# Attention slots of a two-block transformer kernel: outputs read one slot earlier, output units in halves

## What is computed

```python
def even_mixer(...):                       # layer 0; h_lat and h_ctx are 256 rows each
    qa, ka, va, qb, kb, vb = heads(h_lat)  # projections, RMS norms; the same for h_ctx
    qa = rope_2d(qa, row, col)
    ka = rope_2d(ka, row, col)
    o_a = window_attention(qa, ka, va, ka_c, va_c, a_sink)
    o_b = neighbourhood_attention(qb, kb, vb, kb_c, vb_c, b_rpb, rows_n)
    y_lat = jnp.concatenate([o_a, o_b], axis=-1) @ w_out
    ...                                    # y_ctx: the same weights over the context's attention
def odd_mixer(...):                        # layer 1, the latent mixer, no y_ctx
    ...
    y_lat = blockwise_dense_attention(q, k, v, kc, vc, scale) @ w_out
x = x + g1 * y_lat
```

## Time and profile before

| | us |
|---|---|
| runs before: lowest, median, highest of 3 | 2153.28, 2156.61, 2159.62 |
| the profiled execution's own time | 2161.3 |
| its span | 2159.5 |
| TensorE busy | 2067.6 |
| VectorE busy | 1548.4 |
| ScalarE busy | 929.7 |

### The profile page before, as it was taken

One profiled execution on the slowest core, in us unless ns is written; L12 is line 12 of the kernel. 1 busy time (PEld: TensorE's weight loads), 2 busy tenths in 40 slices (PEclk: granted clock), 3 DMA queues, 4 the chain that ended last, 5 costly groups with the idle time before them and its releaser, 6 DMA issues.

```text
span 2159.5 us, 37888 instructions
## 1 busy us (share of the span) xinstructions
PE 2067.6 (96%) x14296; PEld 1767.8 (82%) x14296; DVE 1548.4 (72%) x2708; ACT 929.7 (43%) x1553; POOL 30.0 (1%) x60
## 2 busy tenths in 40 slices
PE   7999999999999999899998889999999999899998
PEld 6889978889889998789975667788887875579987
DVE  7776768776887767888756566767787565767854
ACT  5554645554565544465524444321111234454332
POOL 0000000000000000000000000000000000000000
PEclk9999999999999999999999999999999999999999
DMA  7665525665554642355521111224545522003453
GB/s 277 252 223 186 190 77 196 253 248 167 201 182 167 218 149 98 137 194 180 196 100 59 40 40 62 101 97 156 194 158 210 197 78 81 18 35 124 183 182 139
DMA packets 50513, 326.48 MB, mean 151 GB/s; under 512 B 5360, under 2 KB 8688, under 8 KB 17264
## 3 DMA queue, kind: packets, MB, share of 16 engines
q1 hardware_dynamic: 42480, 266.62, 34.7%
q0 software_dynamic: 7936, 58.53, 7.5%
HBM read 324.07 MB, written 1.05 MB: 151 GB/s over the span
## 4 chain that ended last, share of the span: by engine, by line
PE 82%; DVE 12%; issue 3%; ACT 3%; DVEq 0%; DMA 0%; ACTq 0%; SPq 0%
PE psum L2221 14%; PE psum L2166 9%; PE psum L2167 8%; PE psum L2168 8%; PE psum L2222 7%; PE psum L2278 4%; PE psum L2279 4%; PE psum L2280 4%; PE psum L2774 3%; DVE w_lo L1219 2%; PE psum L2635 1%; PE psum L2775 1%; PE psum L2158 1%; PE psum L2299 1%; ACT w_hi L712 1%
## 5 line engine op out<-in xcount | busy, mean ns | idle before, releaser
L712 ACT ACTIVATE w_hi<-raw 128x1024 fp32r<-128x1024 f32 (+1 forms) x542 | 515.1, 991 | 605.6 <-PE psum L2168 366.3
L1219 DVE TENSOR_TENSOR w_lo<-raw,w_hi 128x1024 fp32r<-128x1024 f32 (+1 forms) x534 | 589.7, 1145 | 158.9 <-ACT w_hi L712 144.8
L2221 PE MATMUL psum<-h_both,w_hi 128*128 128x512 f32 x1344 | 476.5, 399 | 4.8 <-DVE rope_tmp L1269 3.6
L2222 PE MATMUL psum<-h_both,w_lo 128*128 128x256 f32 x1344 | 376.1, 280 | 0.0
L2221 PEld LDWEIGHTS psum<-h_both,w_hi 128*128 128x128 f32 x1344 | 252.3, 188 | 69.1 <-DVE rope_tmp L1269 3.7
L2166 PE MATMUL psum<-h_both,w_hi 128*128 128x256 f32 (+1 forms) x792 | 255.3, 322 | 7.6 <-DVE x_res L1433 2.0
L2222 PEld LDWEIGHTS psum<-h_both,w_lo 128*128 128x128 f32 x1344 | 253.5, 189 | 0.0
L2167 PE MATMUL psum<-h_both,w_hi 128*128 128x256 f32 (+1 forms) x792 | 251.8, 318 | 0.0
L2168 PE MATMUL psum<-h_both,w_lo 128*128 128x256 f32 (+1 forms) x792 | 251.6, 318 | 0.0
L2278 PE MATMUL psum<-g_both,w_hi 128*128 128x256 f32 x704 | 201.8, 287 | 1.2 <-DVE w_lo L1219 1.2
L2279 PE MATMUL psum<-g_both,w_hi 128*128 128x256 f32 x704 | 199.1, 283 | 0.0
(11 more groups left out here) (405 smaller groups left out, 3565.5 us busy)
## 6 DMA issues: line engine op xcount, KB each, us to landing
raw<-in_weights SPq DMA_DIRECT2D x207, 1024.0 KB, 4.8
raw_ada<-in_ada POOLq DMA_DIRECT2D x48, 1024.0 KB, 5.1
raw<-in_weights SPq DMA_DIRECT2D x64, 704.0 KB, 4.1
arena<-in_rpb POOLq DMA_DIRECT2D x1, 2048.0 KB, 12.3
arena<-in_fox_c POOLq DMA_DIRECT2D x1, 1696.0 KB, 9.5
const_region<-in_latent_c POOLq DMA_DIRECT2D x1, 1335.0 KB, 6.1
const_region<-in_even_c POOLq DMA_DIRECT2D x1, 1191.0 KB, 8.4
x_res<-in_x_lat SPq DMA_DIRECT2D x4, 256.0 KB, 7.2
```

Of the source, the lines that this page charges most:

```text
L712: nc.scalar.activation(wh[s][:, a], raw[s][:, a], ACT.Copy).then_inc(hi_ready, 1)
L1219: V.tensor_tensor(wl[s][:, a], raw[s][:, a], wh[s][:, a].bitcast(F32), ALU.subtract).then_inc(lo_ready, 1)
L2221: mm(psum[:, o, :], w_hi, h_both[:, :, k, 0:T], start=k == 0, stop=False)
L2222: ins = mm(psum[:, o, 0:T], w_lo, hh[:, k, 0:T], start=False, stop=k == DC - 1)
```

## The change

Two parts. In the even mixer VectorE's slot k reads the output of step k-2, not k-3; its place between shift and weighing stays. In the latent mixer an output unit is now two entries of the order, `out` with the first 12 matmuls and `done` with the other 12 and the semaphore. Units 0 to 3 stand in halves behind latent slots 11 to 18 (slots 35 to 42). VectorE makes the next panel's low half at `out` and updates the residual at `done`, both now after the weighing of their slot.

```diff
-                      9: (("spread", ("k", 6)),), 11: (("spread", ("k", 7)), ("out", 0)), 13: (("out", 1),),
-                      15: (("out", 2),), 16: (("out", 3),)}
+                      9: (("spread", ("k", 6)),), 11: (("spread", ("k", 7)),)}
             for k in range(19):
                 yield "slot", N_EVEN_STEPS + k
                 yield from behind.get(k, ())
+                if k > 10:
+                    yield ("out", "done")[(k - 11) % 2], (k - 11) // 2
             for q in range(4, 8):
                 yield "out", q
+                yield "done", q
...
                 for what, key in between:
-                    lat_unit(what, key)
+                    if what not in ("out", "done"):
+                        lat_unit(what, key)
                 if k < N_LAT:
                     step_weigh(k)
+                for what, key in between:
+                    if what in ("out", "done"):
+                        lat_unit(what, key)
...
-                if k >= 3:
-                    step_read(k - 3)
+                if 2 <= k < N_EVEN_STEPS + 2:
+                    step_read(k - 2)
...
+            def lat_out(out, s, k, m):
+
+                for kk in range(4):
...
+                    mm(o, w_hi, hh[:, y, 0:T], start=kk == 0, stop=False)
+                    mm(o, w_hi, hl[:, y, 0:T], start=False, stop=False)
+                    ins = mm(o, w_lo, hh[:, y, 0:T], start=False, stop=kk == 3)
+                return ins
...
-                        out = unit()
-                        for m in range(2):
...
-                        ins.then_inc(gemm_done, 1)
+                        out_half = unit()
+                        lat_out(out_half, s, k, 0)
+                    elif what == "done":
+                        lat_out(out_half, s, k, 1).then_inc(gemm_done, 1)
```

More of the change, by code:

```diff
@@ L2100, in lat_unit @@
                     dve.wait_ge(e_roped, 5 + pos.n("l_ropes", 1))
-                elif what == "out":
+                elif what == "done":
                     if k > 5:
@@ L2777, in mlp_latent @@
                 stage(4, 4, 1, 2, out_of)
+            def lat_out(out, s, k, m):
+                for kk in range(4):
+                    if k == 4 and m == 0:
+                        pe.wait_ge(st_y, 16 + 4 + kk + 1)
+                    w_hi, w_lo = wtile(s, kk, 2 * (k % 2) + m, TJ)
+                    y = 4 * (k // 4) + kk
+                    o = out[:, m * T:(m + 1) * T]
+                    mm(o, w_hi, hh[:, y, 0:T], start=kk == 0, stop=False)
+                    mm(o, w_hi, hl[:, y, 0:T], start=False, stop=False)
+                    ins = mm(o, w_lo, hh[:, y, 0:T], start=False, stop=kk == 3)
+                return ins
             def latent():
```

## The result

| | before | after |
|---|---|---|
| runs: lowest, median, highest of 4 | 2153.28, 2158.11, 2162.62 | 2135.60, 2137.98, 2141.38 |
| profiled execution, its span | 2161.3, 2159.5 | 2135.6, 2133.8 |
| ratio to the kernel before, 95% interval | | 0.9904 [0.9878, 0.9929] |

A forecast was written before the change was run, and what follows sets the result against it. TensorE's idle and low-clock stretches were taken as the bound. Even mixer -10.8, latent -3.4 and clock -4.2 gave -18.4 us: 2161.3 to 2142.9, less 4.7 for the slow profiled run, 2138; range 2132 to 2146.

The forecast's parts named there:

- What bounds the kernel: Whole kernel: TensorE, busy 96% of the span; only ending its idle or low-clock stretches saves time.
- Eight waits, -12.3: Even mixer, slots 4 to 14: value products' eight waits for the read of an output go, -12.3 us.
- Cover of 2.2 us: Even slots 4 and 18: weighing still ends 2.2 us or more before the transposes, despite the earlier read.
- New wait of +0.9 in slot 15: Even mixer: transposes in slot 15 newly wait about 0.9 us, shown in the profile after; bounds 0 and 1.1.
- Slot 6, +0.6: Even mixer: the earlier sum of squares in slot 6 meets ScalarE's square, +0.6 us; bounds 0 and 0.6.
- Latent, -3.8 and +0.4: Latent mixer: the 3.40 us wait and a third wait go, -3.8; breaks in four output units cost +0.4.
- Clock, -4.2: Half-clock stretches at 1235.6 and 1918.3, directly behind stalls that go, counted as won: 1.7 and 2.5 us.
- the first and third stretch: Half-clock stretches at 1235.6 (1.7 us) and 1918.3 (2.5 us), both expected to return to full clock.
- The second, counted as kept: Half-clock stretch at 1276.6, expected to stay because the spreads' waits ahead of it stay; 3.1 us more if it went.
- the clock that doesn't come back (2142): Rival, chance 0.15: waits go but low-clock stretches fall elsewhere; -14.2 us, so 2142.
- The displaced wait (2151): Rival, chance 0.06: even mixer's earlier reads make transposes late, eating its 10.8 us; -5.9 remains, so 2151.
- the closed loop (2165): Rival, chance 0.03: in VectorE's order each of 16 even-mixer reads holds the transposes 1.7 us; about +9, so 2165.

The follow-up runs named there:

- even part alone: Kernel before with only the even mixer's read moved, step k-2 in slot k, latent mixer as before; ratio 0.9939 to the kernel before.
- halves alone: Kernel before with only output units 0 to 3 in halves, VectorE's low halves and residual updates still ahead of the weighing; ratio 0.9973.

## Why the prediction was right, step by step

The forecast was 2138 and the median is 2137.98. That it agrees to the digit is luck: the change is worth 20.1 between the medians, not 18.4, and the median before came out at 2158.11 with a fourth run, not 2156.61.

- **What bounds the kernel**: right. Same instructions, same VectorE time, and all of the gain is idle time and clock of TensorE.
- **Eight waits, -12.3**: right in number, place and cause. They go when the read of a step later is done; with the read only moved ahead of the shift six of the eight go and 1.1 us is left.
- **Cover of 2.2 us**: right for the two slots that it was read from (2.25 and 2.45 us in slots 4 and 18), but too wide as a statement on all receiving slots. In the trace after, the room between weighing and transposes is 0.96 us in slot 6, 1.26 in slot 16 and 4.55 in slot 13. A single read fits everywhere, and doubled reads cost 0.8 us in all.
- **New wait of +0.9 in slot 15**: right where the clock is whole (0.87 in the even part alone), hidden in the changed kernel's own trace by a half-clock stretch. So the sign that I named for that trace did not appear there.
- **Slot 6, +0.6**: 0.53.
- **Latent, -3.8 and +0.4**: the waits of transposes in these slots went from 4.6 to 0.8, and the breaks cost 0.39.
- **Clock, -4.2**: the first and third stretch came back, as counted. The third is firm: the latent stretch has 6.8 us at half clock in all three traces with the old latent part and none in the nine others. In the even stretch the sum varies between executions: 6.8 to 10.2 us in the four traces that keep the eight waits, 0 to 3.4 in the five where step k-2 is read once or twice. And once, with halves alone, the first stretch was missing although its wait was there. The second, counted as kept (3.1), was the mis-sized term: of its 6.8 us at half clock 3.4 are left in the trace after, and none with the even part alone. That is worth 1.4 and 3.1 us. With it the even stretch works out: -12.3 + 0.5 - 1.7 - 1.4 = -14.9, measured -14.93; with the even part alone -12.3 + 0.5 + 0.9 - 1.7 - 3.1 = -15.7, measured -15.65. I had argued that the spreads' waits ahead of it stay. They do (2.3 of 2.5 us), but the same waits cost clock in one execution and none in another. So how much of the second comes back is in part luck of the execution.
- **Rivals**: the clock that doesn't come back (2142) did not come about: outside the two stretches 45.4 us ran at half clock before and 43.8 after, in eight pieces (I had written of four) and nine. The displaced wait (2151) and the closed loop (2165) did not come about either. The loop's mechanism is real, though: with three reads per slot more than half of the even mixer's gain is gone, and with four the kernel is slower than before. I had set its threshold at 0.9 us of room and had no price for what happens past it.

TensorE was busy in 1.95 us, with 14 matmuls, ahead of the stretch at 0.50 in the changed kernel. At the same place of the even part alone these counts are the same, and the clock stayed at 1.00:

```profile
1260.76:1264.17 3.41, 1.95 (x14) 1.27 (x14) 2.02 (x4) 0.00 (x0) 0.00 (x0) 1.00 0.00 0
1264.17:1267.58 3.41, 3.01 (x28) 1.81 (x26) 2.27 (x13) 3.04 (x10) 0.00 (x0) 1.00 0.00 0
```

The Trainium skill, "TensorE: Matmul & The Clock Gate", section on the HAM clock gate, says that the monitor runs on its own and does not start with the kernel. These rows would fit that; no run here shows the monitor itself, so why the clock fell in one execution and not in the other stays open.

Left open: whether separate banks for groups 0 to 8 would have done the same. It wasn't tried, since the second bank holds the sums of squares in these slots. Two halves of one bank weren't tried either.

## What to carry to other kernels

Where a consumer waits for a read-out of a shared bank, only the end of the read counts, and any place for it will do that ends before the bank's next use. Whether work may stand in front of an engine's next product is told by the time between that product and its use, not by the engine's total load: here there was room for about one more read per slot (0.9 us), and past it each further microsecond of VectorE's work cost 0.7 to 1.3 us at the end. To read off what a small edit is worth, compare the time between the same two instructions in two traces, with the granted clock beside it.

## What was not expected

- Stalls that bring the clock down cost well over their length. From two reads to four, TensorE's idle time grew by 14.6 us (11.5 of it waits for the weighing), half-clock time from 0 to 23.9 us, and the even stretch by 24.8.
- A slow clock can hide a wait. The trace of the changed kernel shows no wait in slot 15, and its even stretch is 0.72 us longer than in a trace that shows one of 0.87.
- Splitting output units, which put TensorE's work in another place and of VectorE's only the residual update (0.87 us) a slot later, was nearly as good as taking 3.23 us of VectorE's work out of the way (34.84 beside 33.72 us for the latent stretch).
